# Differential attention's query, key and value blocks as direct fp32 matmuls on an x that Pool transposes out of its two parts

## The reference

```python
h = rms_norm(x, mix_norm[l])                       # x * r(row) * gain(column)
proj = h @ in_proj[l]                              # 1024 x 3328 (and 32 more columns in layer 1)
p_rwkv = token_shift(proj[..., :RWKV_COLS], shift_mu[l])   # 1792 columns, to a recurrence
p_diff = proj[..., RWKV_COLS:IN_COLS]              # 1536 columns: q, k, v of differential attention
```

## Time and profile before

| | |
|---|---|
| median of 3 runs | 1944.86 us (1944.83 to 10261.35) |
| the profiled execution, as run | 1950.51 us |
| its span in the trace | 1948.7 us |
| mean granted TensorE clock | 0.972 of full |
| busy: PE, DVE, ACT, POOL | 1832.7, 1523.9, 1198.5, 54.1 us |
| direct kv products (L530) | 123.0 us busy |
| `w_lo` with gain (L419), `w_hi` with gain (L405) | 163.4 and 150.6 us busy |

### The profile page before, as it was taken

How to read it: one execution, slowest core, us unless ns; L and a number is a source line. 1 busy time by engine, 2 the same in 40 slices (tenths; PEclk the granted TensorE clock), 3 DMA queues, 4 the chain that set the end, 5 groups by cost and what they waited for, 6 DMA issues and landing times.

```text
span 1948.7 us, 31880 instructions
## 1 busy us (share of the span) xinstructions
PE 1832.7 (94%) x10685; PEld 1452.9 (75%) x10685; DVE 1523.9 (78%) x2106; ACT 1198.5 (62%) x1616; POOL 54.1 (3%) x90
## 2 busy tenths in 40 slices
PE   6988898999999887998899999999999999999998
PEld 5665566788876665577788888888888888888886
DVE  5874666655568765674799999999999999999997
ACT  4632444555555312552677888778877878878785
POOL 2000000000020000000300000000000000000000
PEclk9999899999999897999899999999999999999999
DMA  8521163466654311451799999999999999999994
GB/s 255 177 89 56 55 211 98 150 188 187 190 165 142 119 45 34 132 170 61 280 372 341 359 379 336 358 359 345 379 337 361 356 352 370 338 366 347 358 371 152
DMA packets 224014, 474.54 MB, mean 244 GB/s; under 512 B 16680, under 2 KB 41400, under 8 KB 223376
## 3 DMA queue, kind: packets, MB, share of 16 engines
q1 hardware_dynamic: 219456, 458.29, 66.8%
q0 software_dynamic: 3472, 13.65, 2.2%
q10 hardware_dynamic: 960, 1.10, 0.2%
HBM read 468.25 MB, written 1.05 MB: 241 GB/s over the span
## 4 chain that ended last, share of the span: by engine, by line
PE 82%; DVE 11%; ACT 3%; DMA 2%; issue 2%; POOL 0%; DVEq 0%; ACTq 0%; POOLq 0%
PE psum L465 22%; PE psum L467 22%; PE psum L466 22%; PE psum L530 4%; PE psum L489 3%; DVE w_lo L419 2%; PE psum L1002 2%; PE psum L1049 1%; DMA SH<-proj 1%; DVE SH L1561 1%; PE psum L893 1%; DVE NB L1532 1%; DVE st L1538 1%; ACT hN L1261 1%; DVE SH L1532 1%
## 5 line engine op out<-in xcount | busy, mean ns | idle before, releaser
L465 PE MATMUL psum<-w_hi,h_hi 128*128 128x512 f32 (+1 forms) x1648 | 653.7, 397 | 31.5 <-DVE w_lo L419 29.5
L467 PE MATMUL psum<-w_hi,h_lo 128*128 128x512 f32 (+1 forms) x1648 | 644.3, 391 | 0.0
L466 PE MATMUL psum<-w_lo,h_hi 128*128 128x512 f32 (+1 forms) x1648 | 644.0, 391 | 0.0
L465 PEld LDWEIGHTS psum<-w_hi,h_hi 128*128 128x128 f32 x1648 | 312.6, 190 | 106.1 <-DVE w_lo L419 27.0
L467 PEld LDWEIGHTS psum<-w_hi,h_lo 128*128 128x128 f32 x1648 | 312.3, 189 | 66.5
L466 PEld LDWEIGHTS psum<-w_lo,h_hi 128*128 128x128 f32 x1648 | 312.9, 190 | 62.7 <-issue 0.5
L419 DVE SCALAR_TENSOR_TENSOR w_lo<-ring,col,w_hi 128x512 fp32r<-128x512 f32 (+1 forms) x232 | 163.4, 750 | 75.2 <-ACT w_hi L405 73.6
L405 ACT ACTIVATE w_hi<-ring,col 128x512 fp32r<-128x512 f32 (+1 forms) x232 | 150.6, 701 | 114.3 <-PE psum L467 109.6
L435 DVE TENSOR_TENSOR w_lo<-ring,w_hi 128x1024 fp32r<-128x1024 f32 x144 | 172.2, 1220 | 7.7 <-ACT w_hi L431 3.2
L431 ACT ACTIVATE w_hi<-ring 128x1024 fp32r<-128x1024 f32 x144 | 151.9, 1060 | 41.1 <-PE psum L467 41.1
L435 DVE TENSOR_TENSOR w_lo<-dproj,w_hi 128x1024 fp32r<-128x1024 f32 x120 | 145.8, 1222 | 17.1 <-ACT w_hi L431 13.0
(11 more groups left out here) (315 smaller groups left out, 2336.0 us busy)
## 6 DMA issues: line engine op xcount, KB each, us to landing
ring<-in_expert_w_gu SPq DMA_DIRECT2D x128, 512.0 KB, 5.4
SH<-in_expert_w_gu SPq DMA_DIRECT2D x120, 512.0 KB, 5.8
proj<-in_expert_w_gu SPq DMA_DIRECT2D x104, 512.0 KB, 6.1
dproj<-in_expert_w_gu SPq DMA_DIRECT2D x72, 512.0 KB, 5.8
dproj<-in_expert_w_down SPq DMA_DIRECT2D x72, 512.0 KB, 5.0
ring<-in_expert_w_down SPq DMA_DIRECT2D x64, 512.0 KB, 5.1
ring<-in_in_proj SPq DMA_DIRECT2D x48, 512.0 KB, 4.4
ring<-in_dense_w_gu SPq DMA_DIRECT2D x88, 256.0 KB, 3.1
```

Of the source, the lines that this page charges most:

```text
L465: pe.matmul(o, h[0], w[0], start=start, stop=False, skip_group_check=True)
L466: pe.matmul(o, h[0], w[1], start=False, stop=False, skip_group_check=True)
L467: return pe.matmul(o, h[1], w[0], start=False, stop=stop, skip_group_check=True)
```

## The change

The twelve blocks of `rest` become direct: they are not split by ACT and DVE, and PE multiplies them in fp32 from the ring. Their left operand is a new fp32 x with the gain, `x_gained(k, t)`, in two tensors: `xg_a` (k 0 to 5, new) and `xg_b` (k 6 and 7, over columns 2048 to 2559 of `h_hi`, which no block of this stage uses). Pool writes it in `gained_x`: for each t one addition and one multiplication of 128x512 for k 0 to 3, and two pairs of 128x256 for k 4 to 7, twelve instructions in a layer. In layer 0 it stands in Pool's queue after the LORA shift and before the R shift; in layer 1 it replaces the four additions, ahead of the DMA of `mu` and the K shift. The 32 columns of layer 1 are multiplied from it too, so DVE no longer scales `vresd_w`. PE waits for `raw_ready` ahead of `rest`.

```diff
+        xg_b = nc.alloc_sbuf_tensor_at("xg_b", [P, 512], F32, offset=h_base + 4 * 2048)
+        xg_a = sb("xg_a", [P, 1536])
...
-            blocks += square_blocks(in_proj[l], chunks_in[0:4], gain=(l, COL["mix"])) + square_blocks(in_proj[l], chunks_in[4:], gain=(l, COL["mix"]))
+            blocks += square_blocks(in_proj[l], chunks_in[0:4], gain=(l, COL["mix"]))
+            blocks += [("direct", src, cw, None) for _, src, cw, _ in square_blocks(in_proj[l], chunks_in[4:])]
...
-                    if src[0] == "mT":
+                    straight = src[0] == "mT" or name[0] == "inb"
+                    if straight:
                         wd = take_direct(cw)
...
+                                lhs = memT[:, kb + k, t * P:(t + 1) * P] if src[0] == "mT" else x_gained(kb + k, t)
+                                last = pe.matmul(banks[c][t][:, 0:cw], lhs, wd[:, k, :],
                                                  start=(kb + k == 0), stop=(kb + k == 7), skip_group_check=True)
...
-                    pe.wait_ge(raw_ready, 4)
-                    pe.wait_ge(side_ready, 1)
+                    pe.wait_ge(raw_ready, 2 * 8)
+                    pe.wait_ge(lw_in, 80)
...
-                            last = pe.matmul(bank[:, 0:VR], hTv[:, k, t * P:(t + 1) * P], vresd_w[:, k, :], start=(k == 0), stop=(k == 7))
+                            last = pe.matmul(bank[:, 0:VR], x_gained(k, t), vresd_w[:, k, :], start=(k == 0), stop=(k == 7))
...
+                pe.wait_ge(raw_ready, 8 * (l + 1))
                 some(rest, 4)
...
+            def gained_x(l):
+
+                gain = col[:, l, COL["mix"]:COL["mix"] + KD]
+                if l == 0:
+                    pool.wait_ge(col_in, 16)
+                n = 8 * l
+                for g in range(2):
+                    for t in range(TT):
+                        B.wait_evacuated(pool, ("hT", l, 0, t, g))
+                        for k0, kn in ((0, 4),) if g == 0 else ((4, 2), (6, 2)):
+                            to = xgs[k0 // 6][:, k0 % 6:k0 % 6 + kn, t * P:(t + 1) * P]
+                            of = [m[:, k0 * SEQ:(k0 + kn) * SEQ].rearrange("p (k t) -> p k t", t=SEQ)[:, :, t * P:(t + 1) * P] for m in (h_hi, h_lo)]
+                            step(pool.tensor_tensor(to, of[0].bitcast(F32), of[1].bitcast(F32), ADD))
+                            n += 1 if kn == 2 else 2
+                            pool.tensor_tensor(to, to, bc(gain[:, k0:k0 + kn].unsqueeze(2), kn, P), MUL).then_inc(raw_ready, 1 if kn == 2 else 2)
+                pool.wait_ge(raw_ready, n)
...
                 if l:
-                    for g in range(2):
-                        for t in range(TT):
-                            B.wait_evacuated(pool, ("hT", l, 0, t, g))
-                            pool.tensor_tensor(part(hT, g, t), part(h_hi, g, t).bitcast(F32), part(h_lo, g, t).bitcast(F32), ADD).then_inc(raw_ready, 1)
+                    gained_x(l)
...
                 shift_in(l, LORA_)
+                if l == 0:
+                    gained_x(l)
...
-                    tt(vresd_w[:, :, :], vresd_w[:, :, :], bc(gains(l, "mix").unsqueeze(2), KD, VR), MUL)
```

More of the change, by code:

```diff
@@ L219, in decoder_trunk, with x_gained @@
         memT = mem_T[:, :].rearrange("p (k t) -> p k t", k=KD)
+        xgs = [m[:, :].rearrange("p (k t) -> p k t", t=SEQ) for m in (xg_a, xg_b)]
+        def x_gained(k, t):
+            return xgs[k // 6][:, k % 6, t * P:(t + 1) * P]
         mu = hN[:, 0:NMU]
@@ L528, in project_steps @@
                         for k in range(2):
-                            if src[0] == "mT":
-                                last = pe.matmul(banks[c][t][:, 0:cw], memT[:, kb + k, t * P:(t + 1) * P], wd[:, k, :],
+                            if straight:
+                                lhs = memT[:, kb + k, t * P:(t + 1) * P] if src[0] == "mT" else x_gained(kb + k, t)
+                                last = pe.matmul(banks[c][t][:, 0:cw], lhs, wd[:, k, :],
                                                  start=(kb + k == 0), stop=(kb + k == 7), skip_group_check=True)
```

## The result

| | before | after |
|---|---|---|
| median of the runs | 1948.43 us (6 runs) | 1961.87 us (1956.58 to 1965.33, 6 runs) |
| ratio | | 1.0067, 95% interval 1.0053 to 1.0080 |
| span of the profiled execution | 1948.7 us | 1961.8 us |
| mean granted clock | 0.972 | 0.976 |
| busy: PE, DVE, ACT, POOL | 1832.7, 1523.9, 1198.5, 54.1 us | 1841.7, 1500.2, 1167.5, 75.4 us |

The changed kernel is 13.1 us slower (10.3 to 15.6), 0.7%, and clear of the noise. A second set of its runs gave 1.0065 (1.0048 to 1.0082). One of the six executions before took 10261.35 us; it stands in the median and not in the ratio.

The account below looks back on a forecast made before the run. PE was taken to bound nearly everywhere, DVE where PE waits for it. +6.0 - 0.7 for passes and splits, +10.0 + 4.5 for Pool beside DVE gave +19.8 us on 1944.9: 1965 us, range 1950 to 1980.

Parts of the forecast that it names:

- the sum: Whole kernel: +6.0 - 0.7 + 10.0 + 4.5 = +19.8 us.
- The base: Median of the runs before the change, 1944.9 us, to which the predicted difference was added.
- Term 1: PE in `rest`: a direct block takes 3.44 us against 2.75 split, so twelve cost 8.3 us a layer.
- that rival: `rest`: direct products could wait for their ring slots; chance 0.02, priced like the rival at 1979 us.
- Term 2: Splits gone from ACT and DVE: waits of 2.3 us vanish, layer 0 nets +6.0 us, layer 1 -0.7 us.
- Term 3: Pool's twelve instructions hold up DVE: +10.0 us in layer 0, +4.5 us in layer 1.
- a DVE instruction with two SBUF operands waits for it whole: While Pool adds or multiplies in SBUF, such a DVE instruction waits for Pool's whole instruction.
- both streams end: Layer 0: DVE and Pool take turns and end at the same sum, keys' product 10.6 - 0.6 = +10.0 us later.
- Layer 1's +4.5 us: Start of layer 1: DVE held up by Pool +3.5 us, mu's DMA +1 us; bounds 2 and 7.
- Pool does not hold DVE up: Pool's instructions slip into gaps or the memset caused the 4.07 us: +5.3 us, 1950 us; chance 0.12.
- Not slower: Pool costs nothing and layer 1 loses its low-clock stretches: kernel ends at about 1941 us; chance 0.07.
- Pool is dearer and PE's clock falls: 128x256 costs up to 1.25 us and waiting PE runs blocks 8 to 11 at half pace: 1979 us; chance 0.19.

Follow-up runs that it names:

- e3: Kernel before with the change in layer 1 alone, layer 0 left as it was; ratio 1.0019 against the kernel before, +3.7 us.
- e2: Changed kernel, but DVE writes the gained x out of PSUM and Pool does no arithmetic there; ratio 1.0009 against the kernel before, +1.8 us.
- e7: Changed kernel with each Pool instruction cut in two halves, 24 in a layer; one execution of 1963.2 us.
- e8: Changed kernel with Pool's work of layer 0 behind the R shift instead of ahead of it; ratio 1.0050 against the kernel before, +9.7 us.
- e9: Changed kernel itself, unaltered, run again as a yardstick; ratio 1.0065 against the kernel before, +12.7 us.
- e11: Changed kernel with layer 0's Pool work behind the R shift and layer 1's mu DMA amid Pool's instructions; ratio 1.0048 against the kernel before, +9.4 us.
- e5: Kernel before with layer 1's blocks direct, DVE writing its gained x from PSUM, no Pool arithmetic there; ratio 0.9989 against the kernel before, -2.1 us.
- e6: Kernel before, blocks still split; DVE writes layer 1's gained x for the 32 columns only, Pool adds nothing; ratio 0.9990 against the kernel before, -2.0 us.
- e1: Changed kernel with the blocks of `rest` kept split, so Pool's work alone; ratio 1.0052 against the kernel before, +10.1 us.

## Why the prediction was right or wrong

The time, 1961.9 us, lies 3.1 us below the predicted 1965 and in the range, and part of that closeness is luck. Against the kernel before it is +13.1 us, where the sum had +19.8, so the sum was 6.7 us too high. The base, 1944.9 us from three executions, was 3.6 us below the 1948.4 us of six, and that hid half of it: from the later base the same sum would have said 1968.2. Nearly the whole excess lies in layer 0: e3 puts layer 1 at +3.7 us, where the sum had +3.8, which leaves 9.4 us for layer 0, where the sum had 16.0. By its own steps:

**Term 1, PE's passes: right where the clock is full.** Nine of the twelve blocks of each layer go at 3.44 to 3.53 us, without a wait for the ring or for `raw_ready` in `rest` (that rival is out), and the four halves at 1.91 us each. The block behind the recurrence's first products took 4.8 us in both layers of this trace, 1.4 us more than forecast, the first 2.5 us of it at the lower of the two clock levels (granted 0.50). That is not a price of direct blocks: the same block takes 3.54 us in both layers of e2, e7, e8, e9 and e11, and in the kernel before the split one of layer 1 took 4.12 instead of 2.9 us.

**Term 2, what ACT and DVE no longer do: it takes away more than was forecast, as far as can be told.** From the mark of the gates' products to the recurrence's first ones layer 0 lost 3.4 us, to 153 us 5.3 us; predicted was +6.0. Of the 5.3 us, 1.4 are the slow clock just named, which leaves 3.9. In whole runs the direct blocks of layer 0, together with DVE's six new instructions there, are the difference of e2 and e5, +0.20% or 3.9 us (their intervals leave 1 to 7). Those of layer 1 are the difference of e5 and e6, -0.1 us and not to be told from zero, where -0.7 was predicted. Between 161 and 207 us the traces of the changed kernel and of e5 both gain some 2 us on the one of before, though e5 changes nothing there: chance, not the change.

**Term 3, Pool and DVE: the right mechanism, layer 0's size wrong.** That it decides is shown by e1 and e2. The price of Pool's instructions was right: 1.25 to 1.32 us for 128x512 and 0.62 to 0.74 us for 128x256, where nothing stretches them, which makes the predicted 10.6 us. The step that failed is "a DVE instruction with two SBUF operands waits for it whole", and with it the size of the sum at which "both streams end": they do end together (51.7 and 52.2 us), some 3.6 us ahead of that sum. The keys' product came 5.3 us later, ended 5.9 us later, and PE's block 11 5.85 us, instead of 10.0. Over the stretch DVE's twelve instructions took 16.6 - (10.5 - 0.6) = 6.7 us longer, 0.56 us for each of Pool's, whose own mean is 0.88 us. So a turn is about 0.3 us shorter than the two instructions alone. With the halves of e7 the same count gives 13.5 - 9.9 = 3.6 us, 0.30 us each, and Pool's instructions that DVE met there were mostly of 0.68 us, then of 0.43: 0.3 us less again. Whose 0.3 us it is the runs don't say. A part looks like DVE's own start: a low part that was held ends 0.56 us after Pool's instruction (563.42 - 562.86 before, 37.90 - 37.34 and 571.21 - 570.65 after), where free ones follow each other at 0.66 us. My rows had a hint of this in them: the low part at 567.17 lasted 1.77 us, 1.1 us more than alone, beside an addition of 1.25 us. I charged the whole one. But the 4.07 us of the same rows were more than the whole, so the rule of 0.3 us less is that of layer 0's stretch, where Pool's additions and multiplications wait for each other and DVE comes in between, and is not shown to hold elsewhere.

Layer 1's +4.5 us held in size: e3 measures +3.7 us (1.0 to 6.6) for the whole layer, with direct blocks that cost nothing that can be told. Its parts were not as told. How soon DVE's K mixing starts after the memset goes by how much arithmetic Pool does ahead of it: 19.5, 20.0 and 19.6 us with none (e2, e5, e6), 23.2 with the four additions of before, 25.5 to 27.8 with the twelve instructions (eight traces). Of mu's DMA, to which I had given 1 us, the traces show 2 us at the transfer and 1.2 us at the K mixing, both in the mean, and the runs nothing clear in the total.

**The rivals.** "Pool does not hold DVE up" is out by e1. "Not slower" is out by the time itself. "Pool is dearer and PE's clock falls": Pool was not dearer. PE's clock fell, but not where it counts there: seven of the twelve matmuls each of blocks 8 and 9 ran at 0.43 us instead of 0.23, after waits of 7.97 and 2.19 us (in the kernel before ten of block 8), and PE then waited for `w_lo` anyway; block 11, the one that lies on the path, ran at full clock. What the slow clock did cost came elsewhere, behind the recurrence's first products (term 1). **What stays open:** what moves the K shift's landing between 8.2 and 10.1 us in the traces with mu right ahead of it, and what share the ring's blocks have; why one low part waits from before Pool's addition is drawn; and whose the 0.3 us of a turn are.

## What to carry to other kernels

Before work is moved to Pool, look at what DVE does in that stretch and whether anything waits for it: 10.6 us of Pool's arithmetic, all of it off the path by itself, cost 5.9 us in layer 0 because DVE's SBUF instructions stood beside it. If the value still lies in PSUM, an instruction of DVE that reads it there costs its own 0.68 us, and such a one was not held up beside Pool (0.68 us at 565.26; 0.68 and 0.67 us in the changed kernel, beside a multiplication that took its usual 1.31 us). If it must be Pool, instructions of half the length held DVE up about half as long in one trace, and Pool itself ended 3 us later. Taking splits off DVE and ACT for slower matmuls can pay only where PE waits for them, and here it did not pay even there: where PE was the bound it cost about 3.9 us, where PE waited it neither cost nor gained anything that the runs can tell.

## What the runs showed of the hardware

- Twelve DVE instructions with two SBUF operands beside Pool's arithmetic were held up by 0.56 us for each of Pool's, whose mean alone is 0.88 us, and by 0.30 us when these were cut in halves. The Trainium skill ("SBUF — State Buffer", section "SBUF: two separate sides") says that the loser "fully blocks" for the whole instruction. The traces agree with the exclusion; in this stretch they show about 0.3 us less than the whole, and for the low part beside two additions in a row 0.9 us more (3.4 us for 2.5 us).
- Pool's memset of one partition, 1.61 us, does not hold DVE up by itself (four low parts in 2.74 us beside it).
- Small DVE instructions of two columns are held up as well where they meet one of Pool's: up to 0.70 instead of 0.16 us.
- A direct product of 128x512 in fp32 is paced at 0.86 us (3.44 us for four), three products of fp32r at 0.69 us (2.75 us for four), both at full clock.
